# Gate and up projections of a SwiGLU layer: two token halves matmul by matmul in two PSUM banks

## The reference

```
def swiglu(h, w_gu, w_down):
    gu = h @ w_gu
    gate, up = jnp.split(gu, 2, axis=-1)
    return (jax.nn.silu(gate) * up) @ w_down

for l in range(DEPTH):                       # DEPTH = 2
    h = rms_norm(x, attn_norm[l])
    x = x + hybrid_mixer(h, w_in[l], ...)
    h = rms_norm(x, ffn_norm[l])
    x = x + swiglu(h, w_gu[l], w_down[l])
```

## Time and profile before

| | |
|---|---|
| time, median of 3 runs | 2898.84 us (2894.78 to 2903.01) |
| span of the profiled execution, first to last instruction | 2891.3 us |
| between that span and the median | 7.5 us |
| mean granted TensorE clock | 0.989 |
| PE busy | 2779.0 us (96% of the span), 13768 matmuls |
| PE weight loads busy | 2299.5 us (80%), 13768 loads |
| DVE, ACT, POOL busy | 1347.7, 862.7, 152.3 us |

### The profile page before, as it was taken

One profiled execution on the slowest core, in us unless ns is written; L12 is line 12 of the kernel. 1 busy time (PEld: TensorE's weight loads), 2 busy tenths in 40 slices (PEclk: granted clock), 3 DMA queues, 4 the chain that ended last, 5 costly groups with the idle time before them and its releaser, 6 DMA issues.

```text
span 2891.3 us, 38682 instructions
## 1 busy us (share of the span) xinstructions
PE 2779.0 (96%) x13768; PEld 2299.5 (80%) x13768; DVE 1347.7 (47%) x2898; ACT 862.7 (30%) x1688; POOL 152.3 (5%) x254
## 2 busy tenths in 40 slices
PE   5999999989999999999989999999899999999998
PEld 5877888777888888888878778878778888888886
DVE  4377666663233333333434776666542333333333
ACT  3222655543211111111032236555441111111110
POOL 2000311100000000000000003111000000000000
PEclk9999999999999999999999999999999999999999
DMA  5211600021111111111041125000212111111111
GB/s 161 77 44 48 155 30 12 17 94 44 57 46 51 44 51 51 44 51 44 0 138 44 44 81 125 19 18 12 104 33 66 51 44 51 44 50 46 48 37 58
DMA packets 212196, 161.44 MB, mean 56 GB/s; under 512 B 52976, under 2 KB 190192, under 8 KB 212080
## 3 DMA queue, kind: packets, MB, share of 16 engines
q1 hardware_dynamic: 204176, 159.93, 18.4%
q10 hardware_dynamic: 7904, 0.04, 0.2%
HBM read 137.27 MB, written 22.66 MB: 55 GB/s over the span
## 4 chain that ended last, share of the span: by engine, by line
PE 45%; DVE 3%; ACT 1%; issue 1%; DVEq 0%; POOL 0%; POOLq 0%; ACTq 0%
PE psum L1433 11%; PE psum L1435 11%; PE psum L1434 11%; PE psum L1519 4%; PE psum L1555 3%; PE psum L1535 2%; PE psum L1484 1%; PE psum L1449 1%; ACT UH L325 0%; DVE X L1313 0%; DVE XN L947 0%; DVE GL L1303 0%; DVE TA L1192 0%; DVE GT L1300 0%; DVE T L1044 0%
## 5 line engine op out<-in xcount | busy, mean ns | idle before, releaser
L1433 PE MATMUL psum<-HH,UH 128*128 128x512 f32 x1856 | 743.1, 400 | 1.3 <-ACT VB L725 1.3
L1435 PE MATMUL psum<-HH,UL 128*128 128x512 f32 x1856 | 723.0, 390 | 0.0
L1434 PE MATMUL psum<-HL,UH 128*128 128x512 f32 x1856 | 723.0, 390 | 0.0
L329 DVE TENSOR_TENSOR UL<-UR,UH 128x1024 fp32r<-128x1024 f32 x116 | 142.0, 1227 | 852.3 <-ACT UH L325 852.3
L1433 PEld LDWEIGHTS psum<-HH,UH 128*128 128x128 f32 x1856 | 348.5, 188 | 86.7 <-issue 12.0
L1434 PEld LDWEIGHTS psum<-HL,UH 128*128 128x128 f32 x1856 | 348.5, 188 | 83.4 <-issue 12.0
L1435 PEld LDWEIGHTS psum<-HH,UL 128*128 128x128 f32 x1856 | 348.4, 188 | 72.7
L1313 DVE TENSOR_TENSOR X<-X,psum 128x512 f32<-128x512 f32 x352 | 236.0, 685 | 147.4 <-PE psum L1435 146.7
L1433 PE MATMUL psum<-PH,GH 128*128 128x512 f32 x704 | 276.0, 392 | 3.0 <-DVE X L1313 3.0
L1434 PE MATMUL psum<-PL,GH 128*128 128x512 f32 x704 | 274.1, 389 | 0.0
L1435 PE MATMUL psum<-PH,GL 128*128 128x512 f32 x704 | 274.0, 389 | 0.0
(11 more groups left out here) (143 smaller groups left out, 3168.3 us busy)
## 6 DMA issues: line engine op xcount, KB each, us to landing
UR<-in_w_gu SPq DMA_DIRECT2D x176, 256.0 KB, 3.1
PR<-in_w_down SPq DMA_DIRECT2D x88, 256.0 KB, 2.9
UR<-in_w_in SPq DMA_DIRECT2D x56, 256.0 KB, 3.2
x_res<-X SPq DMA_DIRECT2D x2, 4096.0 KB, 13.5
PR<-in_w_out SPq DMA_DIRECT2D x32, 256.0 KB, 4.5
X<-x_res SPq DMA_DIRECT2D x2, 4096.0 KB, 14.2
G<-g_d SPq DMA_DIRECT2D x32, 198.0 KB, 2.5
VR<-v_c SPq DMA_DIRECT2D x16, 390.0 KB, 3.6
```

The lines of the kernel that those rows point to most:

```text
L329: nc.vector.tensor_tensor(UL[:, slot, :, :], UR[:, slot, :, :], UH[:, slot, :, :].bitcast(F32), ALU.subtract).then_inc(unit_lo, 1)
L1433: t.matmul(dst, sh, mh, start=start, stop=False)
L1434: t.matmul(dst, sh, ml, start=False, stop=False)
L1435: return t.matmul(dst, sl, mh, start=False, stop=stop)
```

## The change

`gate_up` no longer calls `half_unit` twice. A new function, `both_halves`, goes through the same 48 matmuls of a product in another order: for each feature tile and each of the three parts, half 0 into the one bank and then half 1 into the other. The two products of a pair have the same stationary operand. The waits ahead of it now cover both halves at once: for the silu (or `GT`) of both banks, and in the first chunk of a layer for all 16 steps of `HL`.

```diff
+                def both_halves(slot, dst):
+
+                    for k in range(KD):
+                        for part, (w, h) in enumerate(((UH, HH), (UH, HL), (UL, HH))):
+                            for hf in range(2):
+                                last = t.matmul(dst[hf][:, :], w[:, slot, k, :], h[:, k, 512 * hf:512 * hf + 512],
+                                                start=(k == 0 and part == 0), stop=(k == KD - 1 and part == 2))
+                                if k == KD - 1 and part == 2:
+                                    last.then_inc(stat, 1)
+
...
                     u = QT + 2 * j
                     for gu in range(2):
                         pe.wait_ge(unit_lo, u + gu + 1)
-                        for hf in range(2):
-                            if first and gu == 0:
-                                pe.wait_ge(h_lo, 24 + 8 + hf + 1)
-                            if needed(2 * (j - 1) + hf + 1):
-                                pe.wait_ge(mul_s if gu else silu_s, 2 * (j - 1) + hf + 1)
-                            half_unit(u + gu, gu, hf, bank[2 * gu + hf][:, :], 24 if first and gu == 0 else None)
+                        if first and gu == 0:
+                            pe.wait_ge(h_lo, 24 + 16)
+                        if needed(2 * (j - 1) + 2):
+                            pe.wait_ge(mul_s if gu else silu_s, 2 * (j - 1) + 2)
+                        both_halves(gu, (bank[2 * gu], bank[2 * gu + 1]))
```

## The result

The changed kernel takes 2911.95 us in the median (2906.98 to 2913.59), against 2898.84 before. The ratio is 1.0045, 95% interval 1.003 to 1.0059: slower by 8.7 to 17.1 us. The forecast was 2910.4 us, in 2903 to 2918. The profiled execution has a span of 2905.3 us, 14.0 more than that of before. Its own time is 2906.98, so 1.7 us lie around a span; by that, the profiled execution of before took some 2893.0 us (an estimate). Both are thus 5 to 6 us under their medians, and the two spans can be compared.

What follows compares the result with a forecast made beforehand. TensorE was taken as the bound, busy 2779.0 of 2891.3 us. Order 0, chunk waits 0, hole 8.2 and clock 3.4 us sum to 11.6, added to 2898.84 for 2910.4 us, range 2903 to 2918.

Steps and rivals of the forecast that it cites:

- The new order, 0: Gate and up products: same matmuls and weight loads, pace unchanged at 226.7 ns, so the reordering costs 0.
- vanishing pause: Steps with same weights, other bank: the 13.3 ns beyond the columns vanish at 2112 steps, 28 us faster, 2882; chance 0.06.
- costly change of bank: Gate and up products: every change of bank costs its bound of 1.3 ns, 5.5 us more, 2916; chance 0.06.
- The waits in the chunks, 0: Joint silu and `GT` waits in the chunks: `UH` and `UL` slip 0.49 us, still covered; cost 0.
- The hole, 8.2 us: First gate product of each layer: PE waits for all of `HL`, 4.1 us a layer, paid in full, 8.2 us.
- The clock, 3.4 us: Behind each layer's new hole: half clock slows dense matmuls, 1.7 us a layer, 3.4 us; bounds 0 and 6.8.
- hole without the clock: First gate products: clock stays up, only 8.2 us lost, 2907.0; with a fall in one layer only, 2908.7; together 0.2.
- The sum, 11.6 us: Whole kernel: 0 + 0 + 8.2 + 3.4 us more, 2910.4 us, 0.4% slower; chance 0.65.

Runs made afterwards that it cites:

- experiment 3: Changed kernel, but in each layer's first gate product each feature tile waits only for its own step of `HL` of half 1; 1.0003.
- Experiment 5: Kernel before, old order, with only the joint waits of the chunks for the silu or `GT` of both banks; 1.0002.
- experiments 1: Changed kernel, but each layer's first gate product done the old way, half 0 then half 1 with step-by-step waits; 1.0009.
- experiment 2: Kernel before, old order, but the first gate product waits for all 16 steps of `HL`; 1.0050.
- (6): Changed kernel with six more `HL`-sized steps on DVE ahead of the last `HL` step in each layer; 1.0079, 2920.2 us.
- (7): Kernel before with six more `HL`-sized steps on DVE ahead of the last `HL` step in each layer; 0.9998.
- (4): Changed kernel with 17 extra matmuls per layer, results overwritten, ahead of the wait for all 16 `HL` steps; 1.0036, 2908.4 us.
- experiment 8: Kernel before with 9, 3 and 9 extra float32 matmuls of 512 columns in three holes a layer, results overwritten; 1.0009.

## Why the prediction was right

- **The new order, 0.** Right. The pace is 227 ns in both kinds of steps, the loads are as many as before, and with the hole taken away the new order costs 1.0003 (experiment 3). The rivals of a vanishing pause (28 us faster) and of a costly change of bank (5.5 us slower) both fall with the pair rows and with that ratio, whose interval is -1.7 to +3.5 us. The 215.7 ns that the Trainium skill (TensorE: Matmul & The Clock Gate, section on the 56 ns gap) gives for 512 columns back to back were reached in no kind of step here; the measured 227 ns decides for this kernel.
- **The waits in the chunks, 0.** Right. In the changed kernel's timeline of ACT both silus stand back to back and `UH` comes behind the two:

```profile
1114.77 1.09 ACT L895 ACTIVATE SI<-psum 128x512 f32<-128x512 f32 x2 [9.50 <-PE psum L1484]
1115.74 1.06 ACT L325 ACTIVATE UH<-UR 128x1024 fp32r<-128x1024 f32 x1
```

  That is 0.97 us from the first silu to `UH`, where the earlier trace rows have 0.49 from the second silu: 0.48 us later behind the gate product, as forecast. No wait of PE in the profile after names `SI`, `GT` or `UL`. Experiment 5 puts the joint waits at 1.0002.
- **The hole, 8.2 us.** Measured 4.21 and 4.23 us, 8.4 together. With the joint wait undone the loss is gone (experiments 1 and 3), the joint wait alone brings it (2), made 4 us longer the hole costs about as much more (6), and the same chain behind the old waits costs nothing (7). This is shown.
- **The clock, 3.4 us.** The fall is shown: half clock in the changed kernel, in 2 and in 6 behind the hole, and none when the hole is filled (4). The rule of the Trainium skill (TensorE: Matmul & The Clock Gate, the table "Why this matters for your kernels") against idle gaps between bursts of matmuls agrees with this. The size varies with the execution: 1.3 us a layer in the changed kernel's profile, 2.7 and 2.8 in that of experiment 2, 2.6 in both layers of 6. So 1.7 was inside, and in the profiled sum the term came out 2.6 instead of 3.4. The traces of 4 and of the changed kernel put it at 1.35 us a layer; the measured times don't separate it, as the interval of 4 meets both values. The rival of a hole without the clock, 8.2 us, lies just under the measured 8.7 to 17.1, and the granted clock of 0.50 behind the hole speaks against it.
- **The sum, 11.6 us.** Holes and slow matmuls make 11.0 us in the profile. The other 3 us of the profile's 14.0 lie in unchanged code, 2.5 of them in the mixers, nearly all where half clock fell otherwise; I had assumed those stretches equal. The medians are 13.1 us apart, and the interval from 8.7 us on covers the sum. That 2910.4 came within 1.6 us of the median is in part luck, since single executions of either kernel lie up to 5 or 6 us from their median.

No version was measurably faster than the kernel before: what the new order could give, a spared load or a shorter pause, does not exist in these traces.

## What to carry to other kernels

Pairing matmuls with the same stationary operand gave nothing here, where each still came with its own weight load (188 ns, beside a pace of 227): count the loads in the profile before counting on it. When two results are made side by side instead of one after the other, look at the first use in each stage: the operands of the second half must be there sooner, and a chain on another engine that was covered by the first half becomes a hole. Waiting tile by tile kept the new order and closed the hole (experiment 3, 1.0003).

## What the runs showed of the hardware

The cost of a matmul beyond its columns, 13 ns at 512 and at 384 columns at full clock, was the same with the same or other weights and with the same or another bank. At half clock it was not there: in experiment 2 the pace is 0.427 us (730.17 to 734.44, ten steps), which is 512 columns at 1.2 GHz and nothing more. A float32 matmul of 512 columns shows as two passes of 0.44 us at full clock (experiment 8, 18 records in 7.94 us for nine matmuls), where an fp32r matmul took 0.227.

Executions of one and the same kernel differ by the clock. Of 27 executions of the kernel before that ran beside experiments 5 to 8, the fastest took 2892.42 us at a mean granted clock of 0.989, the slowest 2903.44 at 0.984, and the others mostly line up between them. That spread of 11 us is nearly as large as the effect measured here, 13.1.
